# Transposed input laid out by partition with the first norm's weights in front, and the first weight block's halves on two queues

## What is computed

```
h = rms_norm(x, mix_norm_g)          # x / sqrt(mean(x^2)) * g
proj = h @ w_in                      # w_in: 1024 x 8708
(qa, ka, va, qb, kb, vb, qc, kc, vc, f_logit, qd, kd, vd, gate_logit) = split(proj)
```

## Time and profile before

| | |
|---|---|
| median of 3 runs | 770.51 us (769.64 to 770.77) |
| the profiled execution's own time | 769.26 us |
| its span, first to last instruction | 767.1 us |
| TensorE busy | 759.5 us, 99% |
| VectorE / ScalarE / GpSimd busy | 586.2 / 408.7 / 53.2 us |
| DMA | 137.28 MB, 179 GB/s on average |
| granted TensorE clock | 1.00 |

### The profile page before, as it was taken

One profiled execution on the slowest core, in us unless ns is written; L12 is line 12 of the kernel. 1 busy time (PEld: TensorE's weight loads), 2 busy tenths in 40 slices (PEclk: granted clock), 3 DMA queues, 4 the chain that ended last, 5 costly groups with the idle time before them and its releaser, 6 DMA issues.

```text
span 767.1 us, 9650 instructions
## 1 busy us (share of the span) xinstructions
PE 759.5 (99%) x3712; PEld 636.5 (83%) x3712; DVE 586.2 (76%) x956; ACT 408.7 (53%) x552; POOL 53.2 (7%) x42
## 2 busy tenths in 40 slices
PE   8999999999999999999999999999999999999998
PEld 6888899888888888888888888888988888888886
DVE  5879798687757877787778838799767777768584
ACT  6765455465647546556554545864665445353430
POOL 0200000000002400000000002541000000000000
PEclk9999999999999999999999999999999999999999
DMA  9953444354345567555565557654133766555601
GB/s 317 389 199 101 147 138 165 123 200 146 137 164 165 165 216 253 189 203 193 191 218 172 180 197 275 219 177 161 56 111 109 236 203 199 185 194 190 213 7 55
DMA packets 68796, 137.28 MB, mean 179 GB/s; under 512 B 2576, under 2 KB 6544, under 8 KB 68240
## 3 DMA queue, kind: packets, MB, share of 16 engines
q1 hardware_dynamic: 68320, 135.44, 52.0%
q10 hardware_dynamic: 432, 1.25, 0.5%
HBM read 135.48 MB, written 1.05 MB: 178 GB/s over the span
## 4 chain that ended last, share of the span: by engine, by line
PE 90%; DVE 6%; ACT 3%; issue 1%; DMA 1%; SPq 0%; ACTq 0%
PE b L668 20%; PE b L670 20%; PE b L669 19%; PE SS L668 4%; PE SS L670 4%; PE SS L669 4%; PE TT L635 3%; PE OO L668 2%; PE OO L670 2%; PE OO L669 2%; DVE wlo L1636 2%; DVE ca L2178 2%; PE b L835 1%; PE SS L782 1%; ACT whi L1167 1%; PE OO L1005 1%
## 5 line engine op out<-in xcount | busy, mean ns | idle before, releaser
L1636 DVE TENSOR_TENSOR wlo<-raw,whi 128x2048 fp32r<-128x2048 f32 (+2 forms) x119 | 270.4, 2273 | 78.8 <-ACT whi L1167 78.0
L1167 ACT CAST whi<-raw 128x2048 fp32r<-128x2048 f32 (+2 forms) x119 | 223.2, 1880 | 123.9 <-PE b L670 81.8
L668 PE MATMUL b<-whi,Ahi 128*128 128x512 f32 (+2 forms) x520 | 206.3, 397 | 0.1
L670 PE MATMUL b<-whi,Alo 128*128 128x512 f32 (+2 forms) x520 | 199.8, 384 | 0.0
L669 PE MATMUL b<-wlo,Ahi 128*128 128x512 f32 (+2 forms) x520 | 199.1, 383 | 0.0
L670 PEld LDWEIGHTS b<-whi,Alo 128*128 128x128 f32 x520 | 97.6, 188 | 19.9
L669 PEld LDWEIGHTS b<-wlo,Ahi 128*128 128x128 f32 x520 | 97.9, 188 | 17.9
L668 PEld LDWEIGHTS b<-whi,Ahi 128*128 128x128 f32 x520 | 97.8, 188 | 17.9 <-ACT gates L1242 0.3
L2037 DVE STREAM_TRANSPOSE hT<-ust 32x256 f32<-32x256 f32 (+1 forms) x192 | 81.5, 424 | 2.8
L668 PE MATMUL b<-whi,Bhi 128*128 128x512 f32 x154 | 60.4, 392 | 0.1
L670 PE MATMUL b<-whi,Blo 128*128 128x512 f32 x154 | 60.0, 389 | 0.0
(11 more groups left out here) (306 smaller groups left out, 1104.3 us busy)
## 6 DMA issues: line engine op xcount, KB each, us to landing
raw<-in_w_in SPq DMA_DIRECT2D x38, 1024.0 KB, 5.0
raw<-in_w_up SPq DMA_DIRECT2D x16, 1024.0 KB, 5.4
raw<-in_w_dn SPq DMA_DIRECT2D x16, 1024.0 KB, 5.0
raw<-in_w_d SPq DMA_DIRECT2D x11, 1024.0 KB, 4.9
raw<-in_w_g SPq DMA_DIRECT2D x10, 1024.0 KB, 5.0
raw<-in_w_u SPq DMA_DIRECT2D x10, 1024.0 KB, 5.0
raw<-in_w_out SPq DMA_DIRECT2D x8, 1024.0 KB, 5.1
raw<-in_w_br SPq DMA_DIRECT2D x4, 1024.0 KB, 5.0
```

The lines of the kernel that those rows point to most:

```text
L668: e.matmul(dst, xh, H[:, kc, c0:ce], start=first and kc == krs[0], stop=False)
L670: ins = e.matmul(dst, xl, H[:, kc, c0:ce], start=False, stop=last and kc == krs[-1])
L1167: e.copy(whi[:, s, 0:m], raw[:, r, 0:m]).then_inc(s_hi, 1)
L1636: e.tensor_tensor(wlo[:, s, 0:m], raw[:, r, 0:m], whi[:, s, 0:m].bitcast(F32), ALU.subtract).then_inc(s_lo, 1)
```

## The change

1. DRAM tensor xt becomes 128 x 2056: for partition p first the 8 values of g_mix, then the eight blocks of 256 values. So one partition's share of several blocks lies in one run, and partitions lie 8,224 B apart.
2. The first transfer of it (264 columns: g_mix and block 0) goes into `PT[:, 0, 0:264]`, not `ys`; g_mix is read from there, and so is block 0 (`xT0`). It is SyncE's first issue.
3. The groups of blocks are now 0; 1; 2-3; 4-7. Block 1 is issued by ScalarE, behind its half of (0,0), in the place of the constants.
4. The identity (128 columns) is issued by SyncE behind (1,3); the constants' tile loses g_mix.
5. ScalarE's half of (0,0) has a semaphore of its own, d_half. VectorE copies the two halves in two instructions, that half first; TensorE waits for both.

```diff
-    for name, w in (("ident", 128), ("g_mix", 8), ("maskF", 256)):
+    for name, w in (("ident", 128), ("maskF", 256)):
...
-    g_mix = cst[:, 128:136]
-    maskF = cst[:, 136:392]
+    maskF = cst[:, 128:384]
+    g_mix, xT0 = PT[:, 0, 0:8], PT[:, 0, 8:264]
...
-    xt_v = xt_d.rearrange("(k p) s -> p k s", p=128)
-    XP = [(0, 1), (1, 2), (2, 4), (4, 6), (6, 8)]
+    XP = [(0, 1), (1, 2), (2, 4), (4, 8)]
+    def load_xt(e, i):
+        a_, z_ = XP[i]
+        if i == 0:
+            e.dma_start(PT[:, 0, 0:264], xt_d[:, 0:264]).then_inc(d_xt[0], 16)
+        else:
+            e.dma_start(xT[:, a_:z_, :].rearrange("p k s -> p (k s)"),
+                        xt_d[:, 8 + S * a_:8 + S * z_]).then_inc(d_xt[i], 16)
...
-        def load_xt(i):
-            a_, z_ = XP[i]
-            e.dma_start(xT[:, a_:z_, :], xt_v[:, a_:z_, :]).then_inc(d_xt[i], 16)
-
+        load_xt(e, 0)
         e.dma_start(raw[:, 0, 0:256], units[0][0][:, 0, 0:256]).then_inc(d_piece[0], 16)
-        load_xt(0)
-        load_xt(1)
         load_piece(0, 1)
-        load_xt(2)
+        load_xt(e, 2)
         load_piece(0, 2)
         load_piece(0, 3)
-        load_xt(3)
+        load_xt(e, 3)
         load_piece(1, 0)
         load_piece(1, 1)
-        load_xt(4)
         load_piece(1, 2)
         load_piece(1, 3)
+        e.dma_start(cst[:, 0:128], cst_d[:, 0:128]).then_inc(d_cst, 16)
...
                 w.wait_ge(s_xh, X["A", k, 0] + 1)
+                if k == 0:
+                    w.wait_ge(s_half, 1)
                 w.wait_ge(s_hi, HALF[i] - 3 + kc)
...
-        e.dma_start(raw[:, 0, 256:512], units[0][0][:, 0, 256:512]).then_inc(d_piece[0], 16)
-        e.dma_start(cst[:, 0:136], cst_d[:, 0:136]).then_inc(d_cst, 16)
+        e.dma_start(raw[:, 0, 256:512], units[0][0][:, 0, 256:512]).then_inc(d_half, 16)
+        load_xt(e, 1)
...
-            e.mul(Ahi[:, k, :], xT[:, k, :], g_mix[:, k:k + 1]).then_inc(s_xh, 1)
+            e.mul(Ahi[:, k, :], xT[:, k, :] if k else xT0, g_mix[:, k:k + 1]).then_inc(s_xh, 1)
...
-        w.wait_ge(d_cst, 16)
         for k in range(8):
             input_hi(k)
...
-        w.wait_ge(d_piece[0], 32)
-        e.tensor_copy(whi[:, 0, 0:512], raw[:, 0, 0:512]).then_inc(s_hi, 1)
-        w.wait_ge(d_cst, 16)
+        w.wait_ge(d_half, 16)
+        e.tensor_copy(whi[:, 0, 256:512], raw[:, 0, 256:512]).then_inc(s_half, 1)
+        w.wait_ge(d_piece[0], 16)
+        e.tensor_copy(whi[:, 0, 0:256], raw[:, 0, 0:256]).then_inc(s_hi, 1)
+        w.wait_ge(s_half, 1)
...
-        "xt": a["x"][0].T
+        "xt": np.concatenate([col(a["mix_norm_g"], 8), a["x"][0].T.reshape(8, 128, 256).transpose(1, 0, 2).reshape(128, 2048)], axis=1)
```

More of the change, by code:

```diff
@@ L256, in build @@
     d_piece = [sem(f"d_piece{i}") for i in range(4 * NPC)]
-    d_xt = [sem(f"d_xt{i}") for i in range(5)]
+    d_xt = [sem(f"d_xt{i}") for i in range(4)]
+    d_half = sem("d_half")
     d_cs0 = sem("d_cs0")
@@ L294, in build @@
     s_warm = sem("s_warm")
+    s_half = sem("s_whi_half")
     def pcol(name, i=0, n=1):
@@ L595, in _ @@
             if i == NRAW + 4:
-                e.dma_start(cst[:, 136:N0], cst_d[:, 136:N0]).then_inc(d_cs1, 16)
+                e.dma_start(cst[:, 128:N0], cst_d[:, 128:N0]).then_inc(d_cs1, 16)
                 e.dma_start(cs1[:, 0:CST["MB"][0]], cst_d[:, N0:N0 + CST["MB"][0]]).then_inc(d_cs1, 16)
@@ L1673, in input_lo @@
             w.wait_ge(s_xh, X["A", k, 0] + 1)
-            e.scalar_tensor_tensor(out=Alo[:, k, :], in0=xT[:, k, :], scalar=g_mix[:, k:k + 1],
+            e.scalar_tensor_tensor(out=Alo[:, k, :], in0=xT[:, k, :] if k else xT0, scalar=g_mix[:, k:k + 1],
                                    in1=Ahi[:, k, :].bitcast(F32), op0=ALU.mult, op1=ALU.subtract).then_inc(s_xl, 1)
-        w.wait_ge(d_piece[0], 32)
-        e.tensor_copy(whi[:, 0, 0:512], raw[:, 0, 0:512]).then_inc(s_hi, 1)
-        w.wait_ge(d_cst, 16)
+        w.wait_ge(d_half, 16)
[3 more added lines that the diff above has]
+        w.wait_ge(s_half, 1)
         for k in range(8):
@@ L2455 @@
     arrays = {
-        "x": a["x"][0], "xt": a["x"][0].T, "w_in": a["w_in"][0], "w_br": a["w_branch"][0].reshape(1024, 1024), "w_out": a["w_out"][0],
+        "x": a["x"][0], "xt": np.concatenate([col(a["mix_norm_g"], 8), a["x"][0].T.reshape(8, 128, 256).transpose(1, 0, 2).reshape(128, 2048)], axis=1), "w_in": a["w_in"][0], "w_br": a["w_branch"][0].reshape(1024, 1024), "w_out": a["w_out"][0],
         "w_up": a["w_up"][0], "w_dn": a["w_down"][0], "w_in2": a["w_in_2"][0], "w_out2": a["w_out_2"][0],
@@ L2460 @@
         "w_d2": a["w_down_2"][0],
-        "par": par, "par2": par2, "cst": np.concatenate([ident, col(a["mix_norm_g"], 8), tables], axis=1), "tw": _shifts(a["dw_w_2"][0]),
+        "par": par, "par2": par2, "cst": np.concatenate([ident, tables], axis=1), "tw": _shifts(a["dw_w_2"][0]),
     }
```

## The result

The changed kernel takes 777.31 us (median of 4 runs, 775.89 to 777.72) against 770.2 us for the kernel before; the ratio is 1.0087, 95% interval 1.0072 to 1.0102. It is slower by 7.1 us, where 0.3 us faster was forecast. Its profiled execution took 777.26 us, 8.0 more than that of before (769.26).

What follows compares the result with a forecast made beforehand. TensorE was taken as the bound, limited at chunk 2 by the DMA stream. The gain is the smaller of TensorE's side (0.29 us) and the stream's (0.28): 0.28 us, forecast 770.2 us, range 769.1 to 771.4.

Steps and rivals of the forecast that it cites:

- Identity: Its transfer, now behind piece (1,3), arrives by about 12 to 13 us, before TensorE needs it at 17.04; costs nothing.
- piece (1,0): Weights for block 4: lands 0.26 us later, at 10.69; block 4 starts 0.08 us earlier, bounds -0.37 to +0.95.
- a gain of 1.16: Rival: the slow DMA stretch near the start vanishes, time 769.35 us; chance 0.25 for wholly or in part.
- a loss of 0.16: Rival: piece (1,0) alone lands late, at its lower bound, time 770.7 us; chance 0.11.
- unit 4: Transfer of the first half of chunk 2: lands 0.28 us earlier through longer input runs; lower bound 0.
- Block 0: First block at the start: TensorE begins near 4.4 us instead of 4.71, worth nothing at the end.
- Block 1: Piece (0,1), its weights, issued and landing 0.47 us earlier; TensorE starts it near 6.77; bounds 0 to about 1.4.
- the rule that the prediction cited: Rows starting off a 256 B multiple fetch extra bytes: 0.16 us on the input, leaving 0.12 of the 0.28 gain.
- The wait of 0.21 us at chunk 2: At 28.84 us a matmul after transposes takes 0.44 instead of 0.23 us, read as TensorE waiting for unit 4.
- TensorE's side of the sum: The 0.21 us wait at chunk 2 plus block 4's 0.08 us shift: 0.29 us gain.
- Slow stretch: DMA from 3.6 to 5.6 us at 186 GB/s, 0.95 us of stream lost; forecast to stay.
- the input's rows at a slow rate: Rival: the 8,224 B pitch makes the input move at 186 GB/s, 2.8 us on unit 4, 773.3 us; chance 0.07.

Runs made afterwards that it cites:

- number 1: The changed kernel with the constants' tile made 8 columns wider again (the realigned kernel): 770.28 us against 770.55 for the kernel before.
- number 2: The kernel before with 32 unused bytes per partition behind the constants' tile, nothing else: 776.49 us against 770.55.
- numbers 2 to 10: Nine variants of the kernel before, each with only unused bytes added in front of or behind tiles: 769.83 to 786.17 us.
- 10: The kernel before with 256 unused bytes per partition behind the constants' tile: 769.83 us against 770.02.
- 13: The kernel before with nine warm-up matmuls instead of six, nothing else: 769.26 us against 770.02.
- 11: The changed kernel with its constants' tile 8 columns wider again and nine warm-up matmuls instead of six: 769.2 us against 770.02 for the kernel before.
- 14: The changed kernel with its constants' tile 8 columns wider again and nine warm-up matmuls, run once more: 769.14 us against 770.02 for the kernel before.
- number 9: The kernel before with 32 unused bytes in front of whi, so everything from whi on moved together: 770.36 us against 770.02.
- 8: The kernel before with 32 unused bytes in front of gates, moving hhi and hlo but not Bhi and Blo: 774.4 us against 769.74.

## Why the prediction was wrong

The step that failed is in the first part, on what bounds the kernel: "the change can only touch those at the start" (TensorE's few gaps), and "I found no other place behind it where TensorE waits for a transfer, and take a shift at 28.8 us to reach the end whole". That looked for waits, and took the durations of 3,712 matmuls as given. The edit that cost 7 us, the constants' tile made 8 columns narrower, has no term in the sum at all. What the runs showed in its place: 1,224 matmuls that TensorE goes through one behind the other took 6 ns longer each, because the tiles that their weights come from had moved by 32 bytes against the tile that streams; the pad of 8 columns takes all of it back (number 1), and 32 bytes without the change bring 5.9 us of it (number 2). Under "Identity" I costed the transfers and the wait and said "it costs nothing"; that the tile's width places everything behind it in memory I did not consider. The list of what would prove the forecast wrong names it in one respect only, a shift at 29 us that is not the shift at the end. That is what happened: 1.1 us at 39 us, 8.0 at the end.

Two slips in the sums change nothing of this. The lower bound for piece (1,0) comes out as -0.40 by its own terms (10.43 + 0.74 + 0.83 against 11.60), not -0.37. And a gain of 1.16 and a loss of 0.16, each with half of a scatter of 1.1 us, give a range of 768.8 to 771.2, not 769.1 to 771.4.

The shifts of some tenths at the start can't be judged from one profile before and one after. In the eleven profiles with the old start (the kernel before and numbers 2 to 10 and 13) the copy of piece (0,1) begins between 6.12 and 7.33 us, that of (1,0) between 9.73 and 11.00, and that of unit 4 between 23.67 and 24.97. In the four with the changed start (the changed kernel, 1, 11 and 14) they begin between 6.10 and 6.38, 10.28 and 10.63, and 23.75 and 24.10. The medians are 6.48 and 6.23, 10.22 and 10.51, 24.22 and 23.99. These lean the way that the forecast had them, but the differences are smaller than the scatter.

By the steps:

**Block 0.** Input: landing forecast at 3.2 to 3.5, measured 3.7 (3.0 us after issue); its activation began at 3.73, 0.42 us earlier than before but not the 0.76 that were forecast (3.9 against 4.66 at its end). A copy of 256 columns was taken as 0.25 us and took 0.29. Wrong for the other half of the weights: 3.7 to 4.0 forecast, 5.06 measured. I had taken the 2.5 to 2.8 us that the first transfers of before took as the price of any first or second one. TensorE stood empty for 1.3 us. I had "all this is worth nothing at the end", and the runs don't show it to be worth more: number 1 has the same late half (block 0 at 5.46) and took 770.28 us. The pace of 0.43 us behind the gap comes in kernels with the old start too (number 9).

**Block 1.** Its copy began at 6.38 instead of 6.48: 0.1 us and not 0.47, inside the bounds. The earlier issue was partly eaten by a longer time to landing, 4.6 us against 4.3; in number 1 the copy began at 6.12.

**Piece (1,0).** Forecast 0.26 later, at 10.69; its copy began at 10.63 against 10.46, 0.17 later. The sum of the two effects, more bytes ahead and longer runs, has the right sign and size, as far as the scatter allows; neither was measured by itself.

**Unit 4.** Forecast 0.28 earlier; its copy began at 24.10 against 24.43, 0.33 earlier, and at 23.95 in the realigned kernel. That it comes so near to the forecast is luck, by the scatter above. For the same reason the rule that the prediction cited from the Trainium skill ("DMA: Bandwidth & Descriptors", "How a descriptor splits into AXI transactions"), which would have left 0.12, is neither borne out nor refuted here. The wait of 0.21 us at chunk 2, on which TensorE's side of the sum rests, belongs to the one execution that I read it from. The matmul behind the same transposes takes 0.23 or 0.24 us in every other profile, and in numbers 8, 10 and 13, which have the old start and reach chunk 1 at 17.08 to 17.26 us (17.04), there is no such wait either. So number 1's lead of 0.25 us at 38 us does not show the forecast gain.

**Slow stretch.** It was neither kept nor gone. Both kernels moved about the same from 1.0 to 5.6 us (193 and 196 GB/s). In the changed one 276 GB/s from 2.6 to 3.4 us (365 before), but 255 GB/s from 4.2 to 5.0 (161 before).

**The side that came.** A loss too large to be missed had a chance of 0.06, and for another reason (the input's rows at a slow rate, 773.3 us). That rival did not occur: from 1.0 to 24.4 us the DMA engines moved 352 GB/s after and 346 before. The realigned kernel's 770.28 us lie inside the range, but the forecast's 0.3 us are too small to be told from nothing, so this doesn't confirm its mechanism. The 7 us are a mechanism that stood among no rivals.

## What to carry to other kernels

A change in the width of any tile moves every tile behind it, so after such an edit compare the mean duration of the matmuls group by group (by the tile loaded as weights and the tile that streams), not only the waits: a busy TensorE can still get slower. For matmuls like these (fp32r, 128x128 weights, 512 columns) keep the distance in SBUF between the tile loaded as weights and the tile that streams a multiple of 256 bytes, with a pad where a tile has another width, and give the pad a comment. At the start let the warm-up reach until the data is there; here three more matmuls were worth 0.8 us, and the reordering of transfers nothing that could be measured. And before building a sum on a wait of some tenths in one profile, look for the same wait in a second one.

## What the runs showed of the hardware that was not expected

- A matmul with 128x128 weights and 512 columns of fp32r takes 0.227 us from start to start when the two SBUF operands lie a multiple of 256 bytes apart, and 0.232 to 0.235 us at every other distance tried (32, 64, 96, 128 and 224 bytes modulo 256). The price does not grow steadily with the offset (it is the same at 32 and 64, and least at 128), and doesn't depend on where either tile starts by itself (number 9). What in the chip does this was not tried. The weights' offsets inside a tile were always multiples of 512 bytes here; other offsets, other types and shapes are open.
- After six warm-up matmuls and an idle stretch of 0.5 to 1.9 us the first matmuls ran at 0.43 us in seven profiled executions of thirteen kernels, and at about 0.3 us or less from the third matmul on in the other six. It costs 1.2 us at 38 us (numbers 9 and 10), and would explain much of a scatter of 2 us between runs; with nine warm-ups, in numbers 11, 13 and 14, the scatter is 0.9 to 1.3 us. Whether the gap or the shorter work before it brings the pace of 0.43 was not separated, and what decides between the two paces after the same gap is open.
- SyncE's second transfer took 3.4 to 4.4 us to land with the new input layout, whichever transfer it was, and 2.8 to 2.9 with the old one; the cause is open.
